# Gated scan of a two-block forward pass: the next pair's gates are computed under the present pair, and seven units of the next weight stream run beside the scan's norm

## What is computed

```
def gla_direction(q, k, v, gk, strict):           # chunks of 64 tokens
    b = jnp.cumsum(gk, axis=2)
    b_last = b[:, :, -1]
    b_ref = b[:, :, GLA_CHUNK // 2:GLA_CHUNK // 2 + 1]
    scores = einsum('bnihk,bnjhk->bnhij', q * jnp.exp(b - b_ref), k * jnp.exp(b_ref - b))
    o_intra = einsum('bnhij,bnjhv->bnihv', where(mask, scores, 0.0), v)
    u = einsum('bnchk,bnchv->bnhkv', k * jnp.exp(b_last[:, :, None] - b), v)
    # states: state * exp(b_last) + u, chunk after chunk
    o_inter = einsum('bnchk,bnhkv->bnchv', q * jnp.exp(b), states)
    return o_intra + o_inter

def gla_mixer(q, k, v, g, lr, gk_w, gk_b, norm_g):
    gk_fwd = log_sigmoid(lr[..., :GLA_RANK] @ gk_w[0] + gk_b[0]) / GLA_GATE_NORM
    gk_bwd = log_sigmoid(lr[..., GLA_RANK:] @ gk_w[1] + gk_b[1]) / GLA_GATE_NORM
    o = gla_direction(q, k, v, gk_fwd, False) + flip(gla_direction(flip(q), ..., flip(gk_bwd), True))
    o = rms_norm_2(o, norm_g) * silu(g)
```

## Time and profile before

| | us |
|---|---|
| median of 3 runs | 3972.32 (3963.68 to 3975.25) |
| the profiled execution | 3979.63 |
| span in its trace | 3977.8 |
| TensorE busy | 3636.5 (91%) |
| VectorE busy | 2025.2 (51%) |
| ScalarE busy | 1542.3 (39%) |
| GpSimdE busy | 274.0 (7%) |

### The profile page before, as it was taken

The page is one execution under the profiler, slowest core; times in us unless marked ns, Lnnn a source line. Parts: engine busy times, 40 slices in busy tenths (PEclk is TensorE's granted clock), DMA queues, the critical chain, the costliest instruction groups (busy, mean ns, idle before and its releaser), DMA issues. The chain is left out here.

```text
span 3977.8 us, 73937 instructions
## 1 busy us (share of the span) xinstructions
PE 3636.5 (91%) x32796; PEld 2991.4 (75%) x32796; DVE 2025.2 (51%) x3453; ACT 1542.3 (39%) x2586; POOL 274.0 (7%) x311
## 2 busy tenths in 40 slices
PE   6889989999998998989989798889999999999998
PEld 3576666767676676767678688756989799999887
DVE  1344454444445447674565545656544455555444
ACT  1333343333333333354444344334443444444343
POOL 0001110101011113021000000100000000000000
PEclk8899999999999999999999799989999999999999
DMA  9523333242433406443224343333554545555554
GB/s 316 181 77 94 91 101 111 71 124 75 120 98 94 124 20 249 138 138 106 94 94 167 128 152 124 117 106 124 164 189 147 161 160 186 184 181 180 187 186 156
DMA packets 349484, 548.76 MB, mean 138 GB/s; under 512 B 11724, under 2 KB 119916, under 8 KB 346988
## 3 DMA queue, kind: packets, MB, share of 16 engines
q1 hardware_dynamic: 346860, 539.83, 42.2%
q10 hardware_dynamic: 2304, 4.20, 0.3%
HBM read 535.86 MB, written 8.13 MB: 137 GB/s over the span
## 5 line engine op out<-in xcount | busy, mean ns | idle before, releaser
L300 PE MATMUL lane<-r,r 128*128 128x256 f32 (+1 forms) x8520 | 1509.5, 326 | 35.2 <-DVE r L258 23.1
L300 PE MATMUL bank<-r,r 128*128 128x512 f32 (+2 forms) x6360 | 1413.8, 361 | 38.9 <-DVE r L258 30.3
L258 DVE TENSOR_TENSOR r<-ring,r 128x1024 fp32r<-128x1024 f32 x773 | 949.1, 1234 | 964.3 <-ACT r L297 963.0
L300 PEld LDWEIGHTS lane<-r,r 128*128 128x128 f32 x8520 | 1267.6, 191 | 208.4 <-DVE r L258 31.0
L300 PEld LDWEIGHTS bank<-r,r 128*128 128x128 f32 x6360 | 1055.3, 195 | 255.7 <-issue 61.3
L297 ACT ACTIVATE r<-ring 128x1024 fp32r<-128x1024 f32 x773 | 811.7, 1056 | 997.6 <-PE lane L300 585.7
L300 PE MATMUL lane<-arena 64*64 64x64 f32 (+5 forms) x13708 | 670.9, 251 | 64.7 <-issue 20.1
L300 PEld LDWEIGHTS lane<-arena 64*64 64x64 f32 (+3 forms) x13708 | 507.8, 140 | 213.9 <-issue 122.7
L297 ACT ACTIVATE arena<-lane 128x256 f32<-128x256 f32 (+3 forms) x578 | 252.6, 457 | 569.9 <-PE lane L300 466.3
L269 DVE COPY arena<-lane 128x256 f32<-128x256 f32 (+2 forms) x366 | 132.1, 362 | 315.0 <-PE lane L300 312.0
L258 DVE TENSOR_TENSOR arena<-arena 128x256 f32<-128x256 f32 (+6 forms) x546 | 254.1, 496 | 27.3 <-ACT arena L297 14.6
(11 more groups left out here) (93 smaller groups left out, 1335.9 us busy)
## 6 DMA issues: line engine op xcount, KB each, us to landing
ring<-in_mod_w SPq DMA_DIRECT2D x96, 1024.0 KB, 5.4
ring<-in_w_gate_up SPq DMA_DIRECT2D x88, 1024.0 KB, 5.1
ring<-in_ev_w_in SPq DMA_DIRECT2D x44, 1024.0 KB, 8.7
ring<-in_w_down SPq DMA_DIRECT2D x44, 1024.0 KB, 5.1
ring<-in_od_w_in SPq DMA_DIRECT2D x40, 1024.0 KB, 5.1
ring<-in_w_in SPq DMA_DIRECT2D x40, 1024.0 KB, 5.1
ring<-in_w_xkv SPq DMA_DIRECT2D x32, 1024.0 KB, 5.2
ring<-in_ev_w_out SPq DMA_DIRECT2D x28, 1024.0 KB, 5.1
```

The lines of the kernel that those rows point to most:

```text
L258: return Nothing() if self.e is None else self.e.tensor_tensor(o, a, b, op)
L300: return Nothing() if self.e is None else self.e.matmul(o, l, r, start=start, stop=stop)
```

## The change

`gl_decay` is cut in two. What follows the scan along time (the four arrays on VectorE, the exponentials on ScalarE) is the new step `gl_spread`. The gate of pair n+1 (`gl_gate`) stands behind `gl_states` of pair n, and its `gl_decay` between the two halves of `gl_out` of pair n. The meeting of all engines at `gl_gate` stays for the first pair alone; in its place VectorE waits in `gl_decay` until ScalarE has read `gbc_` of the pair before (`gl_dc`), and in `gl_spread` until TensorE's last `gl_out` of the pair before (`gl_read`), since `gx` overwrites `sts`. The number of units behind each step is now given by `GLA`, 1.6, 1.6, 1.2, 1.4, 0.9 and 0.9, and 2 behind each `gl_norm`. Behind the last unit of `fill` the weave goes on with seven of the 24 hyena units, ahead of `fence mixers`; 17 remain for the local mixers behind it. Nothing is computed otherwise, and no instruction is added or removed on VectorE, GpSimdE or SP.

```diff
--- before.py
+++ after.py
@@ -26,6 +26,7 @@
 MOD_SHARE = 0.125
 CHORES = (1, 3)
 ATT = (1.3, 1.0, 0.3)
+GLA = (1.6, 1.6, 1.2, 1.4, 0.9)
 PIECE = 2048
 ALPHA = 4.0 ** 0.25
 C1 = -0.5 * float(np.exp(-0.5))
@@ -1200,31 +1201,54 @@
     step("gla_ready")
 
     def gla():
-        for d in range(2):
-            for hp in range(2):
-                i = 2 * d + hp
-                step("gl_gate", d, hp, i, bank(aux))
-                yield
-                step("gl_decay", d, hp, i)
-                yield
-                step("gl_keys", d, hp, i)
-                yield
-                step("gl_scores", d, hp, i, bank(aux), bank(aux))
-                yield
-                step("gl_states", d, hp, i, bank(aux))
-                yield
-                for h in range(2):
-                    for c in range(2):
-                        step("gl_out", d, hp, i, h, c, bank(aux))
-                    yield
+
+        pairs = [(d, hp, 2 * d + hp) for d in range(2) for hp in range(2)]
+
+        def gates(n):
+            if n < len(pairs):
+                step("gl_gate", *pairs[n], bank(aux))
+
+        def decays(n):
+            if n < len(pairs):
+                step("gl_decay", *pairs[n])
+
+        gates(0)
+        yield 1
+        decays(0)
+        yield 1
+        for n, p in enumerate(pairs):
+            step("gl_spread", *p)
+            yield GLA[0]
+            step("gl_keys", *p)
+            yield GLA[1]
+            step("gl_scores", *p, bank(aux), bank(aux))
+            yield GLA[2]
+            step("gl_states", *p, bank(aux))
+            gates(n + 1)
+            yield GLA[3]
+            for h in range(2):
+                for c in range(2):
+                    step("gl_out", *p, h, c, bank(aux))
+                if h == 0:
+                    decays(n + 1)
+                yield GLA[4]
         for tl in range(2):
             step("gl_norm", tl)
+            yield 2
         for j in range(0, 4, 2):
             step("to_mix", "gla", 0, j, bank(aux))
 
-    weave(gla(), fill, 1.1)
     to_hyena = stream([feats("hF0", KT, "w_in_2", W2_H + 512 * n, "uh_in", (n,)) for n in range(3)], st_turn)
-    drain(fill)
+
+    def beside_gla():
+
+        yield from fill
+        for _ in range(KT // 2 - 1):
+            yield next(to_hyena)
+
+    beside = beside_gla()
+    weave(gla(), beside)
+    drain(beside)
     step("fence", "mixers")
     step("local_ready")
 
@@ -1898,7 +1922,8 @@
         pe.here("rtm_read")
 
     def gl_gate(d, hp, i, b):
-        pe.here("gl", i, "pe")
+        if i == 0:
+            pe.here("gl", i, "pe")
         fresh(b)
         pe.wait_ge(*at(f"gkw{d}"))
         pe.wait_ge(*at("lr"))
@@ -1936,7 +1961,7 @@
         for q in range(2):
             o = pe.mm(M.bank[b[0]][64 * q:64 * q + 64, P:2 * P], M.zq[:, h, (2 * c + q) * 64:(2 * c + q) * 64 + 64],
                       M.sts[:, 2 * c + q, :], True, True)
-        o.then_inc(*pe.n(("full", *b)))
+        o.then_inc(*pe.n(("full", *b), ("gl_read", i)))
 
     def to_mix(what, gain, j, b):
         src, waits = {"gla": (M.oacc, [("gl_fin", 1)]), "fnet": (M.fo, [("fo", 0), ("fo", 1)]),
@@ -2580,9 +2605,10 @@
         v.here("gla_ready", "dve")
 
     def gl_gate(d, hp, i, b):
-        v.here("gl", i, "dve")
-        for e in ENGINES:
-            v.wait_ge(*at("gl", i, e))
+        if i == 0:
+            v.here("gl", i, "dve")
+            for e in ENGINES:
+                v.wait_ge(*at("gl", i, e))
         full(b)
         v.ts(M.gk, M.bank[b[0]][:, 0:T], M.vcol("gk_b", d * 2 + hp), None, ADD).then_inc(*v.n(("free", *b), ("gl_gk", i)))
 
@@ -2595,8 +2621,14 @@
         v.ts(M.gk, M.gk, 1.0 / 16.0, None, MUL).then_inc(*v.n())
         own()
         st = -1 if d else 1
+        if i:
+            v.wait_ge(*at("gl_dc", i - 1))
         v.scan(M.gbc_[:, ::st], M.C("scan"), M.gk[:, ::st]).then_inc(*v.n())
-        own()
+
+    def gl_spread(d, hp, i):
+        own()
+        if i:
+            v.wait_ge(*at("gl_read", i - 1))
         g4 = c4(M.gbc_)
         ref, lst = (31, 0) if d else (32, 63)
         refb = g4[:, :, ref:ref + 1].to_broadcast([P, 4, 64])
@@ -3296,9 +3328,10 @@
         a.here("gla_ready", "act")
 
     def gl_gate(d, hp, i, b):
-        a.here("gl", i, "act")
-        for e in ENGINES:
-            a.wait_ge(*at("gl", i, e))
+        if i == 0:
+            a.here("gl", i, "act")
+            for e in ENGINES:
+                a.wait_ge(*at("gl", i, e))
         a.wait_ge(*at("gl_gk", i))
         a.act(M.gab, M.gk, ACT.Abs).then_inc(*a.n())
         own()
@@ -3306,7 +3339,7 @@
         own()
         a.act(M.gab, M.gab, ACT.Ln, bias=1.0).then_inc(*a.n(("gl_ln", i)))
 
-    def gl_decay(d, hp, i):
+    def gl_spread(d, hp, i):
         lst = 0 if d else 63
         a.wait_ge(*at("gl_x", i))
         a.act(M.gx, M.gx, ACT.Exp).then_inc(*a.n(("gl_e", i)))
@@ -3633,7 +3666,8 @@
             g.zero(z).then_inc(*g.n(("gla_zeros",)))
 
     def gl_gate(d, hp, i, b):
-        g.here("gl", i, "pool")
+        if i == 0:
+            g.here("gl", i, "pool")
 
     def gl_norm(tl):
         g.wait_ge(*at("gl_in", tl))
```

More of the change, by code:

```diff
@@ L2906, in vector_program @@
         norm0, norm0_q, h1, h1_done, to_q, to_k, to_v, k_rows, v_rows, q_rows, hn_square, hn_gain, hn_turn, hn_turned, hn_done, scores,
-        values, gate_heads, add_second, attended, norm1, rms, rms_turned, vg_in, gla_ready, gl_gate, gl_decay, gl_keys,
+        values, gate_heads, add_second, attended, norm1, rms, rms_turned, vg_in, gla_ready, gl_gate, gl_decay, gl_spread, gl_keys,
         gl_scores, gl_states, gl_out, gl_norm, us_in, uf_in, local_ready, fn_channels, fn_tokens, sc_conv, sc_root, sc_out,
@@ L3480, in scalar_program @@
         k_rows, v_rows, q_rows, hn_square, hn_scale, k_turned, q_turned, scores, p_turned, gate_heads, attended, norm1, rms,
-        rms_turned, lr_in, lr_turned, qk_in, vg_in, gla_ready, gl_gate, gl_decay, gl_scores, gl_norm, to_mix, us_in, uf_in,
+        rms_turned, lr_in, lr_turned, qk_in, vg_in, gla_ready, gl_gate, gl_spread, gl_scores, gl_norm, to_mix, us_in, uf_in,
         fn_channels, fn_tokens, uh_in, add_x, hy_one, hy_two, hy_taps, hy_sides, hy_filter, hy_rows, hy_there, hy_norm,
```

## The result

| | before | after |
|---|---|---|
| median (7 runs each, in the same comparison) | 3973.74 | 3952.87 |
| lowest and highest of them | 3963.68 to 3981.21 | 3945.47 to 3959.81 |
| the profiled execution, and its span | 3979.63, 3977.8 | 3950.59, 3948.7 |
| first gate's matmul to the first 128x512 product | 246.87 | 225.97 |

The ratio is 0.995, 95% interval 0.9937 to 0.9963: faster by 20.9 us, where 14.7 was forecast. It is where rival (a) put it.

The account below looks back on a forecast made before the run. TensorE was taken as the bound, with 48.2 us of waits and slow clock before; less 26.9 of waits and 6.6 of clock after, 14.7 gained. Against the median 3972.3 that gave 3957.6 us, range 3944 to 3969.

Parts of the forecast that it names:

- rival (a): Whole stretch: no new wait drops the clock, +4.95, gain 19.7, 3952.6 us; chance 0.20.
- The waits: First gate to hyena stage: all TensorE waits remaining after the change, 26.9 us in sum.
- Pair 0: Scan's start: wait ahead of the fifth unit 1.9 us instead of 5.59; the scores then wait for nothing.
- Group ends: Stream group ends in pairs 0 to 2: waits of 2.0, 2.0 and 1.6, sum 5.6 instead of 8.8 us.
- Norm: The two norms behind the scan: two waits of 2.1, 4.2 us instead of 11.63.
- `sc_sum`: Behind the last `sc_conv`: waits for the same GpSimdE square, 1.7 us as before, and keeps its 1.6 slow spell.
- Tail: Hyena stage's start: wait 12.0 us instead of 5.22, as `sc_root`, `sc_out` and first `w_out` splits lose cover.
- The clock: Slow clock behind waits: six even chances at 1.6 each, taken as 5.0, plus `sc_sum`'s 1.6: 6.6 us.
- (b): Whole stretch: every one of the six new waits drops the clock, gain 9.8, 3962.5 us; chance 0.15.
- (c): Scan: gate does not get under the pair, group ends stay 2.94; gain 6.5, 3965.8 us; chance 0.15.
- (e): Hyena stage's start: tail of 13.5 instead of 12.0, takes 1.5 us off, within the range; no chance given.
- (d): Seven places: VectorE becomes the bound, late splits cost 31.9; 17.2 slower, 3989.5 us; chance 0.08.

Follow-up runs that it names:

- e8: Changed kernel with the decay's first instruction issued five times instead of once on VectorE in pairs 1 to 3; median 3959.70, ratio 0.9969.
- e4: Changed kernel with the next pair's decay behind the second half of `gl_out` instead of the first; median 3943.93, ratio 0.9935.
- e5: Changed kernel with the `w_out` stream created ahead of the local mixers, so its first two units are split under the last hyena units; median 3947.03, ratio 0.9935.
- e2: Kernel before, scan and meetings kept, with only the seven early hyena units beside the norm; median 3966.27, ratio 0.9993.
- e3: Changed kernel with the meeting of all engines put back at every gate; median 3949.26, ratio 0.9945.
- e1: Changed kernel without any hyena unit ahead of the fence, gates still under the pair; median 3952.86, ratio 0.9951.
- e6: e5 with local mixers' steps dealt unevenly: half a unit behind Fourier steps, 1.5 behind short-convolution steps; median 3942.25, ratio 0.9923.
- e7: e6 with the decay behind the second half of `gl_out`, as in e4; median 3938.08, ratio 0.9917.

## Why the prediction came out as it did

The direction and the places were right, and the releasers too but for one: the second norm's wait was ended by the norm's last instruction on VectorE, ahead of `to_mix`, and not by a split. The sum was 6.2 too small (14.7 against 20.9). By the medians that is at the edge of what they can tell; by the distance it is about three times the noise. It has two parts.

**The waits, 26.9 expected.** The measured ones sum to 1.63 + 3.17 + 3.59 + 1.05 + 0.23 + 1.50 + 11.86 = 23.0, so 3.9 of the 6.2 is here. The idle time in the distance says the same: 14.7 less than before, where the prediction's 37.8 and 26.9 make 10.9.

- Pair 0, cut by units: 1.9 against 1.63. That the scores then wait for nothing holds in all four pairs, with the thinnest cover of 2 us enough.
- Group ends: 2.0, 2.0 and 1.6 against 1.37, 1.27 and 0.53. This is the term that was most wrongly sized, 2.4 in all. The chain was right in its members, as e8 and e4 show, and wrong in its lengths. The rows of the queue above give 1.04 for the four adds of `gl_out`, 1.71 for the decay and 1.12 for the second split. The sum had 1.3 for the adds, twice the duration of two; 1.84 for the decay, read before where the next instruction waits for its result, while here a split that doesn't wait follows it; and 1.15 for the split. From the first split to the end of the wait are 5.54, where the sum had 5.94. The rest is TensorE's own side, a little longer than counted: unit and `gl_out` take 4.41 there (2368.88 to 2373.29), 4.32 in the sum, and that twice. In pair 2, 0.7 of the 1.1 is VectorE's (7.7 from the first split to the end of the wait, 8.4 in the sum) and 0.4 TensorE's.
- Norm: 2.1 and 2.1 against 1.85 and 1.74. Fence: 0.9 against 1.05. `sc_sum`: 1.7 against 1.50. Small group ends: 0.6 against 0.23.
- Tail: 12.0 against 11.86, the largest single term and the closest. e5 confirms how it is made up. That it is so close is partly luck: in e2, e3 and e8 the same order waits for 5.07 or 5.08 and 5.92, 11.0 together. In the changed kernel's trace the slow clock behind `sc_sum` fell on the first bank of the last unit, and the eviction from which VectorE's convolutions start came 5.4 behind the start of `sc_sum`'s matmuls, where it was 4.4 in e3.

**The clock, 6.6 expected.** TensorE's busy time in the distance fell by 6.2, where 10.4 less 6.6 makes 3.8, so 2.4 of the 6.2 is here. I gave six waits an even chance each of 1.6. One of the six brought the clock down, the 1.74 of the second norm. Its price is in the norm's part of the distance, 19.92 us after and 18.38 in e3_meeting_back, where it did not happen: 1.5. With `sc_sum`'s 1.6, that is 3.1, and the four matmuls of `sc_root` took 1.23 at slow clock, where the prediction counted 0.6 of TensorE's time for them. The step that failed is not the price but the sizes that it was asked for: with waits of 1.3 and 0.5 in place of 2.0 and 1.6, three of the six lay at or below the 1.55 that had not been followed by a slow clock in the scan. At sizes of 2.59 and 2.69, e8 shows the spells that the prediction feared. So rival (a) had the number, but its mechanism, no new wait drops the clock, held for five of the six only; that and the shorter waits together make its sum. (The prediction, where it names 3952.6 first, calls it the second rival; it is (a).)

The Trainium skill (TensorE: Matmul & The Clock Gate, "Why this matters for your kernels") warns of idle gaps longer than about 3 us. The 2.94 before is near that. The runs disagree with it as a bound: slow clock followed waits of 2.59 and 2.69 in e8 and of 2.46 in e2 (0.57 granted over the four microseconds from 2498), and once a wait of 1.74.

With 6.6 less 3.1 the clock's part would be 3.5 and not 2.4. Of the 1.1 between them 0.6 is in the four matmuls of `sc_root`. The rest is not placed, and is less than the 2 by which the tail differs among executions of one order.

**The rivals.** (b) is out by the granted clock, which fell behind one of the six waits. (c) needed group ends of 2.94 and is out by the rows; (e) needed a tail of 13.5. (d), VectorE as the bound, is out too: nowhere does it hold TensorE for more than 1.9 before the tail. But e8 shows how near it is, since each microsecond added to its queue at a group end is a microsecond of the kernel. That e2's part would do nothing measurable was in the ledger of the prediction, 11.63 less 4.2 at the norm against 7 at the tail, and I did not say it there; e2 and e1 say it.

## What to carry to other kernels

When independent work is brought forward to cover a hole, look up what it covered where it was: here seven units closed a hole of 11.6 us (two waits of 3.6 together were left) and cost 6.6 further on, until the steps that they had covered were dealt out anew (e6). Where a wait is ended by an engine's queue, its length is a count of what stands ahead in that queue; moving one short step across the instruction that others wait for (e4) changes the wait by up to that step's length, though the engine is half idle (51% busy). And where differences are below the spread of executions, measure the distance between two landmarks around the change in the trace: in the table it follows the medians within 0.3 us for four of the nine kernels and within about 4 for the others. Cut it into parts as well, since a part that the edit leaves alone tells the noise, and look at the granted clock in a part that differs without a reason in the code.

## What the runs showed of the chip

- **The size of a wait alone does not decide the clock.** The wait of 1.85 at the first norm stands in seven kernels with the same work around it. It was followed by the full clock after, in e3, e4, e5 and e8, and by slow clock in e7 and in e6 (0.68 and 0.50, the rows there). What the waits measured here did, by size: in the scan none up to 1.69 (e2) was followed by slow clock; at `sc_sum` 1.50 was in all five traces that have it, and 1.06 in e6 but not in e7; 1.74 was, once; 1.85 sometimes; 1.94 not; 2.46, 2.59, 2.69 and the 2.94s were. A wait of 2.65 at one place in an earlier stage, with the same work around it in both kernels, did both: the eight transposes behind it took 1.06 in the trace of before and 1.94 in the one of after.

```profile
2038.11 1.06 PE L303 MATMUL lane<-cm,arena 128*128 128x128 f32 x8 [2.65 <-DVE arena L263]
```

```profile
2029.44 1.94 PE L304 MATMUL lane<-cm,arena 128*128 128x128 f32 x8 [2.65 <-DVE arena L264]
```
- **A slow spell ahead of a wait costs nothing.** In e6 the slow clock behind 1.85 ran out into the norm's second wait, which vanished (1.52 in e3); the way from the first wait to the fence was 18.38 in both. Slow clock is paid only where TensorE is what ends last.
- **A VectorE instruction that doesn't wait for the one ahead starts about 0.1 us before that one's end; one that waits for its result starts 0.03 to 0.04 behind it.** In the queue above the split of 1.23 is followed 1.15 later, and the scan along time of 0.69, with a split behind it, 0.60 later; within the decay, where each instruction waits for the last, 0.28 is followed after 0.32 and 0.42 after 0.46. The four copies and adds of `gl_out` do each in turn, 0.31 and 0.21, and take 1.04. Sum starts, not durations, and look at what follows.
- **The same square on GpSimdE (128x256) took 0.61 with VectorE idle and 1.53 with VectorE at a split.** The last one ahead of `sc_sum` is of the first kind in after, e2, e3, e4 and e8 and of the second in before, e1, e5, e6 and e7.
